# Transposed softmax probabilities of three attention heads: 32x32 blocks on VectorE and two transfers in place of TensorE

## The reference

```python
h = rms_norm(x, norm1_g); z = einsum('bsd,dn->bsn', h, w_in)          # q, k, v of both mixers, two gates
# mixer A: 8 query heads of 64, 2 key heads; q and k normed per head and rotated
s = einsum('bqkgd,bskd->bkgqs', qb, k)
p = softmax(s, axis=-1)
o = einsum('bkgqs,bskd->bqkgd', p, v)
# mixer B: dilated windows with ALiBi, 12 heads in 3 groups
x = x + einsum('bsc,cd->bsd', gate_a * ya + gate_b * yb, w_out)
x = x + expert_choice_swiglu(rms_norm(x, norm2_g), ...)               # 16 experts, 64 tokens each
y = rms_norm(x, normf_g)
```

## Time and profile before

| | |
|---|---|
| median of 3 runs | 862.01 us |
| profiled execution | 861.86 us, span 859.8 us |
| PE, DVE, ACT busy | 98%, 44%, 31% |
| granted TensorE clock | 0.998 |
| DMA | 239.19 MB, 278 GB/s over the span |

### The profile page before, as it was taken

One profiled execution on the slowest core, in us unless ns is written; L12 is line 12 of the kernel. 1 busy time (PEld: TensorE's weight loads), 2 busy tenths in 40 slices (PEclk: granted clock), 3 DMA queues, 4 the chain that ended last, 5 costly groups with the idle time before them and its releaser, 6 DMA issues.

```text
span 859.8 us, 10399 instructions
## 1 busy us (share of the span) xinstructions
PE 839.4 (98%) x4197; PEld 513.2 (60%) x4197; DVE 379.3 (44%) x665; ACT 264.1 (31%) x461; POOL 29.0 (3%) x50
## 2 busy tenths in 40 slices
PE   9999999999999999999999999999999998989996
PEld 8898866687878888888534343344433433334343
DVE  6377987797715254427322237223131321321351
ACT  6333876695624233216011010010100101001231
POOL 1050000000000000003000000000000000000010
PEclk9999999999999999999999999999999999999999
DMA  9830112023034234884899999999999999999996
GB/s 285 179 98 2 50 50 98 25 76 109 20 123 143 84 107 144 311 356 180 331 410 425 429 428 426 429 428 427 428 428 427 426 430 428 426 423 429 427 420 265
DMA packets 81490, 239.19 MB, mean 278 GB/s; under 512 B 8102, under 2 KB 63526, under 8 KB 65828
## 3 DMA queue, kind: packets, MB, share of 16 engines
q1 hardware_dynamic: 76016, 235.94, 69.7%
q10 hardware_dynamic: 5284, 2.09, 1.0%
q0 software_dynamic: 144, 0.51, 0.1%
HBM read 235.92 MB, written 2.62 MB: 277 GB/s over the span
## 4 chain that ended last, share of the span: by engine, by line
PE 88%; DMA 8%; DVE 1%; ACT 1%; issue 1%; POOLq 0%; POOL 0%; SPq 0%; DVEq 0%; ACTq 0%
PE psum L1657 21%; PE psum L1169 11%; PE psum L1689 11%; PE psum L1171 11%; PE psum L1170 11%; DMA wslot<-in_w_down 7%; PE psum L1614 3%; PE psum L1708 3%; PE psum L1357 2%; PE psum L1818 2%; PE psum L1326 2%; PE psum L1369 1%; PE psum L1669 1%; PE psum L1175 1%; PE psum L1622 1%; PE psum L1379 1%
## 5 line engine op out<-in xcount | busy, mean ns | idle before, releaser
L1657 PE MATMUL psum<-wslot,xinT 128*64 128x512 f32 x1000 | 221.9, 595 | 3.7 <-DMA wslot<-in_w_up 1.9
L1657 PEld LDWEIGHTS psum<-wslot,xinT 128*64 128x64 f32 x1000 | 69.5, 137 | 141.3 <-issue 131.8
L1689 PE MATMUL psum<-wslot,actT 128*64 128x512 f32 x424 | 95.8, 596 | 4.5 <-DMA wslot<-in_w_down 4.5
L1169 PE MATMUL psum<-hT_hi,w_hi 128*128 128x512 f32 x208 | 82.4, 396 | 0.9 <-DVE oT_lo L1991 0.9
L1170 PE MATMUL psum<-hT_lo,w_hi 128*128 128x512 f32 x208 | 81.2, 390 | 0.0
L1171 PE MATMUL psum<-hT_hi,w_lo 128*128 128x512 f32 x208 | 81.2, 390 | 0.0
L1892 DVE TENSOR_TENSOR w_lo<-w_raw,w_hi 128x1024 fp32r<-128x1024 f32 (+1 forms) x46 | 52.9, 1174 | 44.4 <-ACT w_hi L805 44.3
L1689 PEld LDWEIGHTS psum<-wslot,actT 128*64 128x64 f32 x424 | 29.4, 137 | 60.4 <-issue 58.0
L1101 ACT ACTIVATE actT<-psum 128x512 f32<-128x512 f32 x16 | 9.6, 597 | 171.2 <-PE psum L1669 171.2
L2305 DVE TENSOR_TENSOR x<-x,psum 128x512 f32<-128x512 f32 x48 | 29.7, 681 | 57.0 <-PE psum L1708 57.0
L2295 DVE TENSOR_TENSOR y_lo<-psum,y_hi 64x512 fp32r<-64x512 f32 x28 | 19.3, 689 | 80.4 <-ACT y_hi L1111 80.0
(11 more groups left out here) (285 smaller groups left out, 1306.5 us busy)
## 6 DMA issues: line engine op xcount, KB each, us to landing
wslot<-in_w_up SPq DMA_DIRECT2D x24, 2048.0 KB, 25.0
wslot<-in_w_gate SPq DMA_DIRECT2D x24, 2048.0 KB, 23.9
wslot<-in_w_down SPq DMA_DIRECT2D x22, 2048.0 KB, 22.4
w_raw<-in_w_in SPq DMA_DIRECT2D x34, 512.0 KB, 4.7
wslot<-in_w_up SPq DMA_DIRECT2D x15, 1024.0 KB, 11.0
wslot<-in_w_down SPq DMA_DIRECT2D x15, 1024.0 KB, 27.5
wslot<-in_w_gate SPq DMA_DIRECT2D x14, 1024.0 KB, 11.2
w_raw<-in_w_out SPq DMA_DIRECT2D x8, 512.0 KB, 4.9
```

The lines of the kernel that those rows point to most:

```text
L1169: pe.matmul(out_, s_hi, m_hi, start=(k == 0), stop=False)
L1657: mm = pe.matmul(bank[2 * e + n][CAP * f:CAP * f + CAP, :], xinT[:, HALF * h + k, CAP * e:CAP * e + CAP], wslot[place_of(m)][:, k % PART, ...
L1689: mm = pe.matmul(bank[4 + e][CAP * f:CAP * f + CAP, :], actT[:, e, k, CAP * h:CAP * h + CAP], wslot[place_of(m)][:, k % PART, SEQ * f:SEQ ...
```

## The change

The tiles of heads 0, 2 and 4 (u = 0 to 3, 8 to 11, 16 to 19) are *block tiles*, the other twenty *whole tiles*.

- A block tile isn't turned by PE. DVE computes its reciprocal alone; ACT scales the tile in place (`scale_probs(u)`, in ACT's step u + 1); DVE then transposes it in blocks of 32x32 (`turn_blocks(u)`, in DVE's step u + 2) into `blocks`, 8 KB a partition.
- When a head's four tiles are there, SP writes `blocks` to memory (`turned_rows`, 1 MB) and reads it back into the even place of `pT` in four transfers of 32 partitions (`move_blocks`). It does so ahead of the strips 18, 21 and 23 in its own queue. The rows that come back have the queries in the order (block, class, position); ACT writes the odd heads' tiles into `pT` in the same order, and `read_o` and `low_o` put the output back in order of tiles.
- The value products of the first three pairs move from the steps 9, 17, 25 to 11, 19, 26, and wait for the transfers too. `read_o` moves to 12, 20, 27.
- `far` is copied in DVE's step NA + 1 instead of ahead of mixer B's first tile; the first tiles read the piece of `dist` itself.

```diff
+    blocks = sb("blocks", [NT, NT, P], 96)
+    turned_rows = [nc.dram_tensor(f"turned_rows{h}", (P, NT * SEQ), F32, kind="Internal").ap() for h in BLOCK_HEADS]
...
+        def in_blocks(u):
+            return u < NA and u // NT in BLOCK_HEADS
+        def whole_before(u):
+            return sum(not in_blocks(v) for v in range(u))
+        def blocks_before(u):
+            return u - whole_before(u)
+        def wait_blocks_out(eng, n):
+            eng.wait_ge(blocks_moved, 16 * (1 + NT) * n + 16)
+        def wait_blocks_in(eng, n):
+            eng.wait_ge(blocks_moved, 16 * (1 + NT) * (n + 1))
         def wait_probs_free(eng, u):
             before = u - 3 if u < NA else max(u - 3, NA - 1)
-            if before >= 0:
-                eng.wait_ge(probs_turned, before + 1)
+            if before >= 0 and in_blocks(before):
+                eng.wait_ge(blocks_turned, blocks_before(before + 1))
+            elif before >= 0:
+                eng.wait_ge(probs_turned, whole_before(before + 1))
+        def turned_bank(u):
+            return tp[(0, 3)[whole_before(u) % 2]]
+        def block_rows(first, end):
+            return pT[first:end, 0, :, :].rearrange("p k n -> p (k n)").rearrange("p (q n) -> p q n", q=NT)
+        def token_order(i, rows):
+            if i >= OA:
+                return rows
+            return rows.rearrange("p (q c s) -> p c q s", q=NT, c=NT)
+        def by_tiles(i, rows):
+            if i >= OA:
+                return rows
+            return rows.rearrange("p (c q s) -> p c q s", q=NT, c=NT)
...
-        O_READ, O_LOW = (10, 19, 26), (11, 21, NA)
+        MOVES_BEHIND = (18, 21, 23)
+        VALUES_AT = (11, 19, 26)
+        O_READ, O_LOW = (12, 20, 27), (13, 21, NA)
...
+            def move_blocks(n):
+                h = BLOCK_HEADS[n]
+                sp.wait_ge(blocks_turned, NT * (n + 1))
+                if n:
+                    wait_blocks_in(sp, n - 1)
+                sp.dma_start(turned_rows[n], blocks[:, :, :, :].rearrange("p q k s -> p (q k s)")).then_inc(blocks_moved, 16)
+                wait_blocks_out(sp, n)
+                if h >= 2:
+                    sp.wait_ge(pv_done, h // 2)
+                rows = turned_rows[n].rearrange("(q s) (g n) -> g s q n", q=NT, g=NT)
+                for kq in range(NT):
+                    sp.dma_start(block_rows(SQ * kq, SQ * kq + SQ), rows[kq]).then_inc(blocks_moved, 16)
             load_x(0)
             for n in range(len(strips)):
+                if n in MOVES_BEHIND:
+                    move_blocks(MOVES_BEHIND.index(n))
...
-                act_.wait_ge(probs_turned, u + 1)
-                last = act_.activation(pT[:, head % 2, :, cols],
-                                       tp[(0, 3)[u % 2]][:, :].rearrange("p (k i) -> p k i", i=P), ACT.Copy)
+                act_.wait_ge(probs_turned, whole_before(u + 1))
+                if head < A_HEADS:
+                    dst = pT[:, head % 2, :, :].rearrange("p k (q c s) -> p k q c s", q=NT, c=NT)[:, :, :, c, :]
+                    src = turned_bank(u)[:, :].rearrange("p (k q s) -> p k q s", k=NT, q=NT)
+                else:
+                    dst = pT[:, head % 2, :, cols]
+                    src = turned_bank(u)[:, :].rearrange("p (k i) -> p k i", i=P)
+                last = act_.activation(dst, src, ACT.Copy)
                 if u >= NA:
                     last = act_.activation(pT_dil[:, head % 2, :, cols],
                                            tp[1][:, 0:2 * P].rearrange("p (g i) -> p g i", i=P), ACT.Copy)
                 last.then_inc(pT_done, 1)
+            def scale_probs(u):
+                act_.wait_ge(probs_normed, u + 1)
+                p = probs_of(u)[:, 0:SEQ]
+                act_.activation(p, p, ACT.Copy, scale=column(rinv, u)).then_inc(probs_scaled, 1)
             def read_o(i):
                 act_.wait_ge(pv_done, i + 1)
-                act_.activation(oT_hi[:, i, :], tp[2][:, :], ACT.Copy).then_inc(o_hi_done, 1)
+                act_.activation(by_tiles(i, oT_hi[:, i, :]), token_order(i, tp[2][:, :]), ACT.Copy).then_inc(o_hi_done, 1)
...
+                if u and in_blocks(u - 1):
+                    scale_probs(u - 1)
+                if 2 <= u < NA + 2 and not in_blocks(u - 2):
...
             def turn_probs(u):
+                if in_blocks(u):
+                    return
                 pe.wait_ge(probs_normed, u + 1)
                 if u >= NA:
-                    pe.wait_ge(pT_done, u)
+                    pe.wait_ge(pT_done, whole_before(u))
                     for g in range(2):
                         pe.transpose(tp[1][:, P * g:P * g + P],
                                      probs_of(u)[:, SEQ + P * g:SEQ + P * g + P], ident[:, :])
-                elif u >= 2:
-                    pe.wait_ge(pT_done, u - 1)
+                elif whole_before(u) >= 2:
+                    pe.wait_ge(pT_done, whole_before(u) - 1)
                 for k in range(NT):
-                    t = pe.transpose(tp[(0, 3)[u % 2]][:, P * k:P * k + P],
+                    t = pe.transpose(turned_bank(u)[:, P * k:P * k + P],
                                      probs_of(u)[:, P * k:P * k + P], ident[:, :])
                 t.then_inc(probs_turned, 1)
...
-                pe.wait_ge(pT_done, 2 * NT * (i + 1))
+                pe.wait_ge(pT_done, whole_before(2 * NT * (i + 1)))
+                if 2 * i in BLOCK_HEADS:
+                    wait_blocks_in(pe, BLOCK_HEADS.index(2 * i))
                 if i:
                     pe.wait_ge(o_lo_done, i)
                 kv = 2 * i // (A_HEADS // A_KV)
                 for k in range(NT):
                     for hh in range(2):
+                        rows = block_rows(0, P)[:, :, P * k:P * k + P] if 2 * i + hh in BLOCK_HEADS else pT[:, hh, k, :]
                         mm = pe.matmul(tp[2][HD * hh:HD * hh + HD, :], vA[:, k, HD * kv:HD * kv + HD],
-                                       pT[:, hh, k, :], start=(k == 0), stop=(k == NT - 1))
+                                       rows, start=(k == 0), stop=(k == NT - 1))
                 mm.then_inc(pv_done, 1)
...
-                if u > 1 and u % (2 * NT) == 1:
-                    values_a(u // (2 * NT) - 1)
+                if u in VALUES_AT:
+                    values_a(VALUES_AT.index(u))
...
                 dve.wait_ge(exp_done, u + 1)
+                if in_blocks(u):
+                    dve.reciprocal(column(rinv, u), column(rsum, u)).then_inc(probs_normed, 1)
+                    return
                 settle(dve.reciprocal(column(rinv, u), column(rsum, u)))
                 p = probs_of(u)[:, 0:width]
                 dve.tensor_scalar(p, p, column(rinv, u), None, ALU.mult).then_inc(probs_normed, 1)
+            def turn_blocks(u):
+                head, c = divmod(u, NT)
+                if c == 0 and BLOCK_HEADS.index(head):
+                    wait_blocks_out(dve, BLOCK_HEADS.index(head) - 1)
+                dve.wait_ge(probs_scaled, blocks_before(u + 1))
+                dve.transpose(blocks[:, :, :, SQ * c:SQ * c + SQ].rearrange("p q k s -> p k q s"),
+                              probs_of(u)[:, 0:SEQ].rearrange("p (k q s) -> p k q s", k=NT, q=NT)).then_inc(blocks_turned, 1)
...
+                if u >= 2 and in_blocks(u - 2):
+                    turn_blocks(u - 2)
...
-            dve.wait_ge(dist_in, 16)
-            settle(dve.tensor_copy(far[:, :], dist[:, 0, SEQ:SEQ + 2 * P]))
+            dve.wait_ge(shape_parts_in, 16 * 4)
...
+                        if u == NA + 1:
+                            settle(dve.tensor_copy(far[:, :], dist[:, NT - 1, SEQ:SEQ + 2 * P]))
                         dve.wait_ge(score_done, NA + 2 * (u - NA) + 1)
                         dve.tensor_tensor(dist[:, c, SEQ:SEQ + 2 * P],
-                                          far_two[u % 2][:, 1, :, :].rearrange("p g n -> p (g n)"), far[:, :],
+                                          far_two[u % 2][:, 1, :, :].rearrange("p g n -> p (g n)"),
+                                          dist[:, NT - 1, SEQ:SEQ + 2 * P] if u < NA + NT - 1 else far[:, :],
```

More of the change, by code:

```diff
@@ L56 @@
 KIB = 1024
+SQ = 32
+BLOCK_HEADS = (0, 2, 4)
 COL_A = 0
@@ L278, in encoder_block @@
         probs_turned = sem("probs_turned")
+        probs_scaled = sem("probs_scaled")
+        blocks_turned = sem("blocks_turned")
+        blocks_moved = sem("blocks_moved")
         pT_done = sem("pT_done")
@@ L1906, in _ @@
                 split_lo(n)
-            dve.wait_ge(rope_parts_in, 16 * 3)
+            dve.wait_ge(shape_parts_in, 16 * 3)
             for n, g in enumerate((gq, gk)):
```

16 lines of the change are left out of this document (7 added, 9 removed).

## The result

The changed kernel is slower: 870.87 us (median of 4 runs, 869.57 to 873.57) against 862.06 (861.97 to 862.17), ratio 1.0098 [1.0078, 1.0117]. Forecast were 859.7 and a range up to 863.8. The profiled execution took 873.57, with a span of 871.4.

What follows compares the result with a forecast made beforehand. PE bounds mixer A's stage; a weights stream at full rate sets the end. Terms: -0.3 + 3.5 + 1.3 - 1.0 + 0.3 - 1.5 = 2.3 us won, so 859.7, range 856.3 to 863.8.

Steps and rivals of the forecast that it cites:

- The round trip: Each block head's megabyte out to memory and back: 11.0 us; head 4's return, beside dist, makes its product wait 1.5.
- landings over 6.5 us a megabyte: Sign named beforehand that the forecast would be wrong: transfers taking over 6.5 us a megabyte to land.
- rival C: Round trip late from slow memory, 15.6 us: waits of 4.0, 1.7, 6 at value products; 870; decisive past 3.8; chance 0.15.
- Head 0 wins nothing: Mixer A's first block head: DVE is already late, so PE's saved transposes win nothing; 0.3 us lost as a whole.
- A new wait of PE for DVE: Sign expected in mixer A: PE newly waits for DVE at head 0's end, next whole tile not turned before 98.3.
- Heads 2 and 4 win: Mixer A: eight transpose groups leave PE, worth 3.5 us, and 1.3 us of old waits go.
- The tail loses: Mixer A's end, third value product one tile later: 1.0 us of new PE waits, range 0 to 2.
- The copy of far: Between the mixers' stages: far's copy moves behind the operation for which PE resumes; 0.3 us won.
- What DVE and ACT get: Per block tile: DVE's transpose at 0.60 us replaces scaling at 0.40; ACT's scaling is even with the copy it loses.
- rival A: Transfers in time and DVE transpose at 0.40: 4.6 us won, up to 6; 856 to 857.9; chance 0.20.
- Rival D: The weights' stream starts bound by something other than PE, so the end stays at 862.0; chance 0.04.
- What PE wins before 248 us starts the whole stream earlier by the same amount: Late weights' stream: its transfers wait for places PE has finished with, so PE's earlier gain passes through in full.

Runs made afterwards that it cites:

- b3: Changed kernel with head 2 alone by blocks, heads 0 and 4 whole, value products in their old tiles, dist where it was: 865.93 us.
- b1: As a1, but each head's megabyte returns in one transfer to 128 partitions by 8 KB; mixer A's output not the reference's: 862.14 us.
- a1: Changed kernel with dist issued by ACT in its step 28 instead of 24: 866.43 us.
- b2: Changed kernel with heads 2 and 4 alone by blocks, dist issued late, head 4's store ahead of the strip: 863.82 us.
- a2: Changed kernel with 70 identity products on PE ahead of the third value product's wait for the transfers: 877.74 us.
- b4: Changed kernel with identity products filling PE's waits, 8 in head 0 and 32 before head 4's value product: 869.18 us.
- a3: Changed kernel with heads 0 and 2 alone by blocks, second value product in step 18, third in 25: 863.72 us.
- a4: Changed kernel without the round trips and the waits for them; mixer A's output not the reference's: 862.57 us.
- c3: Kernel before the change, with only the third value product and its reading one tile later: 865.42 us.
- d1: As b2, with each head stored in two halves and each half's returns behind its own store: 863.85 us.
- d2: As d1, with the third value product at tile 25 and its reading in 26: 864.41 us.
- d3: As b3 (head 2 alone by blocks), with out and back by halves: 862.86 us.
- c2: As b2, but quarters go straight from SBUF to SBUF in 16 transfers a head, and the third value product is at tile 25: 867.49 us.

## Why the prediction was wrong

*The step that failed is "The round trip".* It said "11.0 us", and "Sharing costs between 0.5 and 3; I put the wait at 1.5 us". The wait measured is 7.8. What was available was right: the last block was turned at 136.0, PE came to the product at 147.3, 11.3 us against the 11.4 forecast (both points 2.5 us later than forecast, since less had been won before them). The trip took 19.1; "landings over 6.5 us a megabyte", a sign named beforehand, is there. Of the 8.1 too many, by the runs:

- 0.7 are in the trip undisturbed (b3: 11.7), and two errors cancel in that. The store takes 3.9, less than the 5.0 of a megabyte coming in the earlier trace rows. The return takes 7.8, because four transfers to 32 partitions by 2 KB move slower than one to 128 by 8 KB (b1: 4.8). Whether it is the partitions or the pieces of 2 KB was not told apart. I had named the 32 partitions as a point for rival C and then priced the return by a row with 128.
- 1.5 are the store's (5.4 against 3.9; in a1 it was 2.7). The strip beside it is not all of it: b2's store without a strip ahead takes 4.8. In both kernels a packet of the instruction queue runs beside this store, and none beside any store of 3.9. By this about 0.9 would go with that packet and 0.6 with the strip; no experiment took the packet away.
- 5.9 are dist beside the return (13.7 against 7.8; a1, without it, has 7.7). I had seen that they meet, and bounded the sharing by 3 with no row behind it. The two could simply have been added for an upper bound, 14.0: dist alone takes 6.3, and both use the same DMA engines, at a share of 1.06. The price varies from one execution to the next: the return takes 11.0 us in a2 (dist issued 1.1 us ahead of it) and 11.3 in b4, so 3.2 to 5.9 in three executions.

*A term was missing: the clock.* Behind a long stop PE works at half the granted clock: 2.9 us at the product (b4 gives them back), about 1.0 in head 0. With the wait that makes 10.7 at this place, where the sum had 1.5.

*"Head 0 wins nothing" was right in kind, not in size.* "A new wait of PE for DVE" came where forecast, with tile 4 at 98.96, not before 98.3. The loss was 1.8 against 0.3. In a3 and b4, where the clock stayed up, tile 7 is turned 17.68 us from the first maximum: so DVE costs 0.9 there, and the clock the other 1.0. The step that was wrong in DVE's part is that PE's slack would take 0.5 of the fourth transpose: in a3 tile 4 is turned 0.3 us later than before (10.82 against 10.54), near the 0.2 forecast, and tile 5 already 0.9 later (13.74 against 12.88), behind a wait of 0.23 for DVE.

*"Heads 2 and 4 win" was slightly high:* 4.0 measured (a4), 4.8 in the sum.

*"The tail loses" was low:* 1.0 in the sum; c3 has 1.8 with `far` as it was, the changed kernel 1.4 with `far`'s 0.3 against it. The range given, 0 to 2, held it, and c3 confirms the cause.

*"The copy of far" was right:* 0.3 (b3: 3.1 behind at tile 26, 2.8 at mixer B).

*What DVE and ACT get was nearly right:* 0.63 start to start against 0.60 for the transpose. ACT's scaling, taken as even with the copy, is 0.12 longer, and the only wait for it is one of 0.4 on DVE.

*Rival C names the right mechanism and the right side, and its 870 is right by chance.* It had waits at all three products from a slow memory. There was one, and memory wasn't slow: the store, at 3.9, was the quick half. The Trainium skill's warning (DMA: Bandwidth & Descriptors, on the fixed cost, in its section on transfers that GpSimd issues) of delays "especially when the write target is HBM", which rival C leaned on, does not show in this store; no run here splits off the receipt itself. C's threshold was too high: it put the turning point at 3.8 us of waits, the sum without its transfers. Without the trip only 0.8 us is won at mixer B (a4), or 1.7 where the clock stays up (b1), and the trips of 11.4 to 12.5 with 0.9 to 2.5 us of wait (b2, d1, d2) all end at or a little over the time of before. Two slips in the working change nothing: 4.6 below 862.0 is 857.4, not rival A's 857.9, and C's third wait comes to 5.7 us by its own terms (15.6 - 11.4 + 1.5), not 6.

*Rival D falls for losses and stays open for gains.* "What PE wins before 248 us starts the whole stream earlier by the same amount" held at the stage's beginning (415.11 in b1, 416.51 before). From there to its last product the profiles have 416.4 us (before), 416.7 (a4), 417.7 (changed), 417.8 (b1), 417.9 (a3) and 418.2 (b2), in no order of their starts. A late start goes through: a2 begins the stage 17.9 us later than the kernel before and ends it 18.3 later. But 1 to 2 us come and go there from one execution to the next, and a gain of 1 us can't be followed through it: b1 begins 1.4 earlier and comes to the last product 0.1 earlier.

## What to carry to other kernels

A transfer that is needed at a known time should be priced by a row of its own form (partitions and bytes a piece), and what the two queues issue within its time should be added to it as an upper bound, not allowed for by a guess. In this kernel a wait of 2.4 us or more on TensorE cost more than itself, since the work behind it ran at half clock for a time, and one of 2.0 us did so in some executions; filler products in the wait give that back (3.9 us here), though not the wait. And when work is taken from the busiest engine, look for the steps that move with it: here one product moved by one tile ate 1.8 us, nearly half of the 4.0 that the 32 transposes of heads 2 and 4 saved.

## What the runs showed of the hardware

- VectorE's transpose in blocks of 32x32, 128x512 f32 within SBUF: 0.698 us, as long as its operations on 512 elements out of PSUM (0.68 to 0.69); its output is written permuted.
- ScalarE's scaling of 128x512 f32 from SBUF to SBUF in place takes 715 ns, its copy out of PSUM 594, with rows permuted in runs of 32 elements or not.
- 1 MB out of SBUF to memory: 3.9 us; 4.8 with a packet of the instruction queue beside it (b2), 5.4 to 6.6 with that and a strip of 512 KB issued 1.8 us ahead. 1 MB back: 4.8 to 4.9 us as 128 rows of 8 KB, 7.6 to 7.8 as four times 32 partitions by 2 KB, 11.0 to 13.7 beside 1.5 MB on the other queue.
- Sixteen transfers of 64 KB between places of SBUF: 2.0 us each from issue to landing, but 0.63 for each issue on SP.
- The same stop of 2.0 us on TensorE brought half clock in some executions (0.66 granted over 99 to 104 us) and none in others (a3, b1: 1.00). Stops of 0.9 to 1.3 us before a value product left it at 3.65 us (b2, d1, d3), stops of 2.4 to 3.5 made it 5.35 (a1, b3, c2, d2), and the one of 7.8 made it 6.57.
